# A two-part transformer block in one kernel: first units of both gated feed-forwards on unnormed chunks, grid attention with split values, cross attention with four score banks

## What is computed

```python
def modulate(h, shift, scale):
    return h * (1.0 + scale[:, None, :]) + shift[:, None, :]

def swiglu(h, w1, w3, w2):
    return (jax.nn.silu(h @ w1) * (h @ w3)) @ w2

for layer in range(2):
    mod = silu(c) @ ada_w[layer] + ada_b[layer]            # six vectors of 1024
    sh1, sc1, g1, sh2, sc2, g2 = jnp.split(mod, 6, axis=-1)
    h = modulate(rms_norm(x), sh1, sc1)
    y = pool_attention_mixer(h, ...) if layer == 0 else mlstm_mixer(h, ...)
    x = x + g1[:, None, :] * y
    h = modulate(rms_norm(x), sh2, sc2)
    x = x + g2[:, None, :] * swiglu(h, ffn_w1[layer], ffn_w3[layer], ffn_w2[layer])

# grid attention, in pool_attention_mixer: 8 query heads of 64, 2 key/value heads
s = einsum('bkgqd,bksd->bkgqs', q_blk, kt) * scale         # 128 queries x 512 keys
p = jax.nn.softmax(s, axis=-1)
o = einsum('bkgqs,bksd->bkgqd', p, vt)
# beside it: pooled means of 4 windows times w_pool; [pool, attention] @ w_out

# cross attention: 4 heads of 256
p = jax.nn.softmax(einsum('bshd,bmhd->bhsm', q, k) / sqrt(256), axis=-1)
o = einsum('bhsm,bmhd->bshd', p, v)
```

## Time and profile before

| | |
|---|---|
| median of 3 runs | 2150.06 us |
| lowest, highest | 2149.21, 2152.73 us |
| the profiled execution | 2150.77 us, of which the span is 2149.1 us |
| mean granted clock of TensorE | 0.983 of full speed |
| busy share of TensorE (matmuls), its weight loads | 97%, 79% |
| busy share of VectorE, ScalarE, GpSimd | 53%, 34%, 41% |
| DMA | 233 MB, mean 109 GB/s |

### The profile page before, as it was taken

How to read it: one execution, slowest core, us unless ns; L and a number is a source line. 1 busy time by engine, 2 the same in 40 slices (tenths; PEclk the granted TensorE clock), 3 DMA queues, 4 the chain that set the end, 5 groups by cost and what they waited for, 6 DMA issues and landing times.

```text
span 2149.1 us, 26665 instructions
## 1 busy us (share of the span) xinstructions
PE 2076.9 (97%) x10222; PEld 1695.0 (79%) x10222; DVE 1134.0 (53%) x1894; ACT 728.9 (34%) x985; POOL 878.2 (41%) x472
## 2 busy tenths in 40 slices
PE   6999899999999999998999999999999999999998
PEld 5877688888888888775578888887897777888887
DVE  4344565636878895468557665704665743111112
ACT  5343533324423223345533222123253333222121
POOL 2322432744444444333234444444445333444442
PEclk8999999999999999999999999999999999999999
DMA  4322202424455543330045555422332022223322
GB/s 139 109 74 85 69 1 79 142 93 136 139 176 196 175 160 96 98 104 29 12 155 167 196 171 182 136 89 69 118 120 89 30 79 79 98 88 102 100 81 79
DMA packets 225160, 233.26 MB, mean 109 GB/s; under 512 B 4227, under 2 KB 220116, under 8 KB 224924
## 3 DMA queue, kind: packets, MB, share of 16 engines
q1 hardware_dynamic: 224672, 231.70, 33.3%
q10 hardware_dynamic: 380, 0.11, 0.0%
HBM read 229.55 MB, written 2.24 MB: 108 GB/s over the span
## 4 chain that ended last, share of the span: by engine, by line
PE 86%; DVE 7%; ACT 2%; issue 2%; DMA 1%; POOL 1%; ACTq 0%; DVEq 0%
PE ps L2118 21%; PE ps L2120 21%; PE ps L2119 21%; PE ps L2167 6%; PE ps L2172 3%; PE ps L2805 2%; PE ps L2819 1%; PE ps L2274 1%; PE ps L2533 1%; POOL wL L593 1%; DVE hnL L1338 1%; DMA raw<-in_w_xkv_dram 1%; PE ps L2464 1%; ACT wH L725 1%; DVE T L1351 1%
## 5 line engine op out<-in xcount | busy, mean ns | idle before, releaser
L593 POOL TENSOR_TENSOR wL<-raw,wH 128x1024 fp32r<-128x1024 f32 (+2 forms) x322 | 773.8, 2425 | 1106.1 <-ACT wH L725 1088.7
L725 ACT ACTIVATE wH<-raw 128x2048 fp32r<-128x2048 f32 (+2 forms) x161 | 302.5, 1879 | 473.0 <-PE ps L2120 352.2
L2118 PE MATMUL ps<-hnH,wH 128*128 128x512 f32 x1152 | 455.9, 396 | 4.3 <-POOL wL L593 4.3
L2120 PE MATMUL ps<-hnH,wL 128*128 128x512 f32 x1152 | 449.9, 391 | 0.0
L2119 PE MATMUL ps<-hnL,wH 128*128 128x512 f32 x1152 | 448.9, 390 | 0.0
L2118 PE MATMUL ps<-uH,wH 128*128 128x512 f32 x712 | 281.8, 396 | 4.2 <-DVE uL L1336 1.8
L2120 PE MATMUL ps<-uH,wL 128*128 128x512 f32 x712 | 278.9, 392 | 0.0
L2119 PE MATMUL ps<-uL,wH 128*128 128x512 f32 x712 | 278.5, 391 | 0.0
L1710 DVE SCALAR_TENSOR_TENSOR adacc<-adaw,small,adacc 128x256 f32<-128x256 f32 x336 | 267.5, 796 | 12.3 <-DVE adacc L1710 0.3
L2118 PEld LDWEIGHTS ps<-hnH,wH 128*128 128x128 f32 x1152 | 217.1, 188 | 49.1 <-issue 5.7
L2120 PEld LDWEIGHTS ps<-hnH,wL 128*128 128x128 f32 x1152 | 216.5, 188 | 45.9
(11 more groups left out here) (413 smaller groups left out, 3021.7 us busy)
## 6 DMA issues: line engine op xcount, KB each, us to landing
raw<-in_ffn_w_dram SPq DMA_DIRECT2D x60, 1024.0 KB, 5.3
adaw<-in_ada_w_dram SPq DMA_DIRECT2D x48, 1024.0 KB, 7.3
raw<-in_w_dram SPq DMA_DIRECT2D x32, 1024.0 KB, 5.2
raw<-in_w_in_dram SPq DMA_DIRECT2D x14, 1024.0 KB, 5.5
raw<-in_od_w_in_dram SPq DMA_DIRECT2D x12, 1024.0 KB, 5.4
raw<-in_w_xkv_dram SPq DMA_DIRECT2D x8, 1024.0 KB, 5.4
raw<-in_ffn_w_dram SPq DMA_DIRECT2D x8, 768.0 KB, 4.3
raw<-in_ev_w_in_dram SPq DMA_DIRECT2D x5, 1024.0 KB, 5.4
```

The source lines that it names most:

```text
L593: nc.gpsimd.tensor_tensor(wL[n % 2][:, k0:k1, 0:c], raw[n % 2][:, k0:k1, 0:c], wH[n % 2][:, k0:k1, 0:c].bitcast(F32), ALU.subtract).then_i ...
L725: nc.scalar.activation(wH[n % 2][:, 0:kc, 0:c], raw[n % 2][:, 0:kc, 0:c], ACT.Copy).then_inc(w_hi, 1)
L2118: nc.tensor.matmul(out_ap, wh, xh, start=first, stop=False)
L2120: return nc.tensor.matmul(out_ap, wl, xh, start=False, stop=last)
```

## The change

Three parts, joined.

**Both gated feed-forwards.** The first unit (w1, columns 0 to 255) is multiplied with x (1 + scale), not normed, in `hnH` and `hnL`, made during the last units of `ev_out` or `od_out` (`raw`). The norm's sums and its broadcast run inside the unit. The shift's part of the product, shift @ w1, is kept apart: VectorE multiplies and adds the raw w1 unit over its eight chunks with the shift (`shift_products`, into `wacc`), TensorE sums over partitions into `ps[7]` (`shift_sums`, between the last two blocks of the stage before), and ScalarE adds it as the bias of Silu (`fconst`). The blocks are multiplied by the inverse root in `ssum`. SyncE waits for the products before it loads unit 2 into the same buffer. Normed chunks go to `uH`, `uL`, hidden ones to `hnH`, `hnL`. The loops over i are written out on SyncE, ScalarE, VectorE and TensorE. One piece of the conditioning moves from `ff2_0` into `ev_out`, and its sums are ordered anew.

**Grid attention.** Probabilities stay without their inverse sums; they are split into `gpH` (ScalarE) and `gpL` (VectorE, out of PSUM); the values are split too (`gvp`, padded with zeros to 128 columns), so that a value product is three fast matmuls over 128 columns, two heads adding into one bank. Inverse sums of two heads at a time are copied out by GpSimd (`gsx`), transposed by TensorE, copied by ScalarE (`gsc`), and VectorE multiplies the pair's output with them (`gout`).

**Cross attention.** Four score banks; scores wait for the exponential of step g - 4, and the first output product waits for the last one.

Tiles are placed anew for it (left out below). The diff, cut:

```diff
+SUMS_STEP = (11, 21, 29, 35)
+SUMS_BANK = (3, 0, 0, 3)
...
+CROSS_SCORES = (4, 5, 1, 2)
...
+                if layer == 0:
+                    load_ada(1, 0, 0)
+                for u in range(24):
+                    if u == 2:
+                        sp.wait_ge(wc_done, layer + 1)
+                    load(n0 + u)
+                    if layer == 0 and u < 11:
+                        load_ada(1, 0, u + 1)
+                    if layer == 0 and u >= 12:
+                        load_ada(1, 1, u - 12)
...
+            for half in range(2):
+                nc.gpsimd.memset(gvp[:, half, :, 0:64].bitcast(F32), 0.0)
+                nc.gpsimd.memset(gvp[:, half, :, 128:192].bitcast(F32), 0.0)
+                nc.gpsimd.memset(gvp[:, half, :, 256:320].bitcast(F32), 0.0).then_inc(g_pad, 1)
...
+                pool.wait_ge(g_inv, o + 1)
+                if o:
+                    pool.wait_ge(g_bc, o)
+                nc.gpsimd.tensor_copy(gsx.rearrange("p (i h c) -> p i h c", i=TB, h=2),
+                                      hrs[:, 8 * o:8 * o + 8].rearrange("p (h i x) -> p i h x", h=2, x=1).to_broadcast(
+                                          [P, TB, 2, 64])).then_inc(g_sx, 1)
+
+            inverse_sums(0)
             g = 0
             for grp, w in enumerate(WINDOWS):
+                if grp == 3:
+                    inverse_sums(1)
...
+                    if 0 <= t < ns:
+                        h, i = t // TB, t % TB
+                        act.wait_ge(tp_done, step0 + t + 1)
+                        if i == 0 and h >= 2:
+                            act.wait_ge(pv_done, ATT["grid"]["pv0"] + h - 1)
+                        nc.scalar.activation(gpH[h % 2][:, :, i * P:(i + 1) * P],
+                                             ps[6 + (step0 + t) % 2][:].rearrange("p (j t) -> p j t", j=TB),
+                                             ACT.Copy).then_inc(pt_done, 1)
+                    if s < ns:
+                        act.wait_ge(mx_done, g + 1)
+                        act.wait_ge(tp_done, g - PR_RING + 1)
+                        m = g % PR_RING
+                        nc.scalar.activation(pr[m][:], ps[4 + g % 2][:], ACT.Exp, bias=nmax[:, m:m + 1],
+                                             accum_out=hstat[:, s:s + 1]).then_inc(ex_done, 1)
+                    if s - 1 in SUMS_STEP:
+                        o = SUMS_STEP.index(s - 1)
+                        act.wait_ge(g_bc, o + 1)
+                        if o:
+                            act.wait_ge(g_out, o)
+                        nc.scalar.activation(gsc[:], ps[SUMS_BANK[o]][:], ACT.Copy).then_inc(g_sc, 1)
...
+                    if s >= 16 and s % 8 == 0:
+                        o = s // 8 - 2
+                        act.wait_ge(g_out, o + 1)
+                        nc.scalar.activation(uH[:, 4 + o, :], gout[:], ACT.Copy).then_inc(op_hi, 1)
...
+                high(n0 + 2)
+                for c in range(2):
+                    act.wait_ge(r_scaled, 2 * layer + c + 1)
+                    nc.scalar.activation(R[c][:], R[c][:], ACT.Silu, bias=fconst[:, c:c + 1]).then_inc(silu_done, 1)
+                for c in range(2):
+                    act.wait_ge(blk_taken, TAKEN[b0 + 2 + c + 1])
+                    nc.scalar.activation(hnH[:, c, :], T[(q0 + c) % 2][:], ACT.Copy).then_inc(op_hi, 1)
...
+                for i in range(2):
+                    for p in range(1 - i, 4):
...
+            def raw_norm(layer, n, first):
+                name, at = f"ff2_{layer}", layer * 48 + 24
+                highs_and_squares(n, name, BLOCK0[n], first, raw=(Q0[name + "_raw"], hnH, lambda j: modp[:, at + 8 + j:at + 9 + j]))
+                roots(name)
+                norm_highs(Q0[name + "_norm"], lambda j: mod[:, at + j:at + j + 1], to=uH)
...
+                        chain(nc.vector.tensor_reduce(nmraw[:, m:m + 1], ps[CROSS_SCORES[s % 4]][:, 0:M_MEM], AX, ALU.max))
...
+                    if 0 <= t < ns:
+                        h, i = t // TB, t % TB
+                        dve.wait_ge(pt_done, step0 + t + 1)
+                        if i == 0 and h >= 2:
+                            dve.wait_ge(pv_done, ATT["grid"]["pv0"] + h - 1)
+                        if t == TB:
+                            dve.wait_ge(g_ql, 4)
+                        ts = slice(i * P, (i + 1) * P)
+                        nc.vector.tensor_tensor(gpL[h % 2][:, :, ts], ps[6 + (step0 + t) % 2][:].rearrange("p (j t) -> p j t", j=TB),
+                                                gpH[h % 2][:, :, ts].bitcast(F32), ALU.subtract).then_inc(g_pl, 1)
...
+                    if s >= 9 and s % 8 == 1 and s < ns + 8:
+                        o = s // 8 - 1
+                        dve.wait_ge(ex_done, step0 + 8 * o + 8)
+                        if o < 4:
+                            nc.vector.reciprocal(hrs[:, 8 * o:8 * o + 8], hstat[:, 8 * o:8 * o + 8]).then_inc(g_inv, 1)
...
+                    if s >= 15 and s % 8 == 7:
+                        o = s // 8 - 1
+                        dve.wait_ge(pv_done, ATT["grid"]["pv0"] + 2 * o + 2)
+                        dve.wait_ge(g_sc, o + 1)
+                        if o:
+                            dve.wait_ge(op_lo, Q0["ev_mix"] + MIX_OUT[o - 1] + 1)
+                        nc.vector.tensor_tensor(gout[:], ps[1 + o % 2][:], gsc[:], ALU.mult).then_inc(g_out, 1)
...
+            nc.vector.tensor_copy(value_part(0), values_in).then_inc(v_hi, 1)
+            dve.wait_ge(v_hi, 1)
+            nc.vector.tensor_tensor(value_part(1), values_in, value_part(0).bitcast(F32), ALU.subtract).then_inc(v_row, 1)
...
+            grid_attention({0: lambda: take_pool(3), 4: lambda: queries_low(2), 7: lambda: queries_low(3),
...
+                dve.wait_ge(raw_in[n % 2], 16 * (n // 2 + 1))
+                for k in range(KC):
+                    if k == 0:
+                        chain(nc.vector.tensor_scalar(wacc[:], raw[n % 2][:, 0, :], shift(0), None, ALU.mult))
+                    else:
+                        ins = nc.vector.scalar_tensor_tensor(out=wacc[:], in0=raw[n % 2][:, k, :], scalar=shift(k), in1=wacc[:],
+                                                             op0=ALU.mult, op1=ALU.add)
+                        if k < KC - 1:
+                            chain(ins)
+                        else:
+                            ins.then_inc(wc_done, 1)
...
+            residual_and_sums(b, "ff2_0", mcol(mod, 0, 2), raw=(Q0["ff2_0_raw"], hnH, hnL, mcol(modp, 0, 4)),
+                              beside={2: lambda: conditioning(1, 0, 0), 5: lambda: shift_products(0)})
...
+                dve.wait_ge(wc_mm, layer + 1)
+                nc.vector.tensor_copy(fconst, ps[7][:, 0:2])
+                dve.wait_ge(bc_copied, 2 + layer)
+                for c in range(2):
+                    dve.wait_ge(blk_done, b0 + c + 1)
+                    nc.vector.tensor_tensor(R[c][:], ps[(b0 + c) % 4][:], ssum[:], ALU.mult).then_inc(r_scaled, 1)
+                for i in range(2):
                     for p in range(4):
+                        if i == 0 and p == 0:
+                            pair(0, 0)
+                            cond(0, 1)
+                            continue
                         cond(i, 2 * p)
                         cond(i, 2 * p + 1)
                         pair(p, i)
...
+                dve.wait_ge(bc_done, NORMS[name] + 1)
+                nc.vector.tensor_copy(ssum[:], ps[4][:]).then_inc(bc_copied, 1)
+                for _ in normed_steps(name, mcol(modp, layer, 4), Q0[name + "_norm"], mcol(mod, layer, 3), to=(uH, uL)):
...
-                    dst, ts = ps[4 + g % 2][:, 0:M_MEM], slice(i * P, (i + 1) * P)
-                    pe.wait_ge(ex_done, g - 1)
+                    dst, ts = ps[CROSS_SCORES[s % 4]][:, 0:M_MEM], slice(i * P, (i + 1) * P)
+                    pe.wait_ge(ex_done, g - 3)
+                    if s == 2:
+                        pe.wait_ge(blk_taken, TAKEN[BLOCK0[AT["xo"][0]]] - 2)
...
                         unit_ready(n)
+                        pe.wait_ge(ex_done, step0 + ns)
...
+                    pe.wait_ge(ex_done, g + 1)
+                    if t >= 2:
+                        pe.wait_ge(pt_done, g - 1)
+                        pe.wait_ge(g_pl, t - 1)
...
+                    for i in range(TB):
+                        ins = nc.tensor.transpose(ps[SUMS_BANK[o]][:, i * P:(i + 1) * P], gsx[:, i * P:(i + 1) * P], ident)
+                    ins.then_inc(g_bc, 1)
...
+                            pe.wait_ge(g_out, h // 2 - 1)
+                    c0 = h // 4 * P + (64 if h % 2 == 0 else 0)
+                    dst = ps[1 + h // 2 % 2]
+                    first, last = h % 2 == 0 and j == 0, h % 2 == 1 and j == TB - 1
+                    nc.tensor.matmul(dst[:], gvp[:, 0, j, c0:c0 + P], gpH[h % 2][:, j, :], start=first, stop=False)
+                    nc.tensor.matmul(dst[:], gvp[:, 0, j, c0:c0 + P], gpL[h % 2][:, j, :], start=False, stop=False)
```

(57 more changed lines are left out.)

135 lines of the change are left out of this document (102 added, 33 removed).

## The result

The changed kernel takes 2129.5 us, median of four runs (2125.9 to 2131.9), against 2151.1 (2149.2 to 2152.7) for the kernel before: a ratio of 0.9891, 95% interval 0.9873 to 0.9910.

A forecast was written before the change was run, and what follows sets the result against it. TensorE, busy 97% of the span, was taken as the bound. Gated feed-forwards -5.7 and -5.5, grid attention -2.3 and cross attention -1.0 summed to -14.5 us, giving a forecast median of 2135.5 us, range 2129 to 2144.

The forecast's parts named there:

- 32 x (1.00 - 0.68): Grid attention: replacing each float32 value product (1.00 us) by three fast matmuls (0.68) saves 10.2 us over 32 steps.
- the 0.11 of the scores: Grid attention: two score matmuls take 0.57 us instead of 0.45; the excess, a change of kind, only moves to the values.
- the 3 us for the clusters: Grid attention, steps 17 to 21 and 25 to 29: VectorE's work nearly equals TensorE's; 0 to 4 us each, 3 together.
- The start: Start of grid attention: queries moved ahead of a row maximum and a low part waiting for ScalarE cost 2 us (0 to 3).
- the end: End of grid attention: TensorE waits for high and low of the last transposes, not one copy, +0.8 us (0.3 to 1.5).
- Lies in idle time: Values in `ev_in`: their added low part (0.7 us) was claimed to fall in idle time, costing nothing.
- the cover: `ev_out`: shift products ready by 1101, asked for by TensorE at about 1102.4, leaving 1.4 us; lateness cost taken as 0.
- the term 25.74: Gated feed-forwards: the stretch of `ff1` in us, taken whole with its 1.1 us stall as base for both new stretches.
- (b): Rival: grid attention gains all of its matmul time, -7.8 us, giving 2130; chance 0.13.
- (a): Rival: VectorE bounds the grid attention clusters, so grid attention gains nothing or loses, +0 to +4, 2138 to 2142; chance 0.20.
- (c): Rival: the first unit does not cover the norm, half the gain of both feed-forwards stays, about 2141; chance 0.12.
- (d): Rival: slower than before; grid attention's 32 subtractions take 2.9 us instead of 0.7 beside GpSimd, 2164; chance 0.05.

## Why the prediction was wrong

*The grid step.* The step that failed is the term 32 x (1.00 - 0.68) for grid attention. It priced the product's own rows, moved the 0.11 of the scores to the values, and let the rest of the old step stand. The moving was right (0.46 and 0.79 forecast, 0.46 and 0.78 measured). The transposes, left at 0.53, take 0.35, and that is the 0.19 by which the step was off: it fell by 0.51 us and not by 0.32. What the runs show in its place: the old step carried a price of 0.34 us that hangs on a float32 product with 64 output rows and that its neighbours pay in part, so that it leaves with the product. The transposes take 0.53 us before such a product, 0.43 before a float32 one of 128 rows and 0.35 before a fast one. The rows had a sign of it: in the old step the last transpose takes 0.20 us to the next matmul and the three ahead of it 0.11 each.

*Where the 6 us of grid attention lie.* In the middle: from the start of the ninth step to the last score 52.4 us became 43.2, -9.2, where the forecast's terms make -2.8 there (23 value products of 0.32, three of the four broadcasts, the 3 us for the clusters). Of the difference, 23 x 0.19 = 4.4 us are the step. The start was right: the first eight steps went from 15.0 to 16.8 us, +1.8, with +2 forecast less one value product. So was the end, from the last score: 10.20 to 9.39, -0.8, where the forecast's terms make -1.2; TensorE's gaps there come to 1.2 us, 0.8 was taken.

*The clusters.* I allowed 3 us for VectorE at steps 17 to 21 and 25 to 29. A step with a pool product takes 2.45 us, 0.86 over its neighbour, as before (2.96 over 2.10): no loss. One step outside them, with the end of a head and `gout`, lost 0.8. The 3 were too many by about 2.

*The values' low part.* "Lies in idle time" was wrong. TensorE waits for it before a product of the head norms (L2915, idle 0.49):

```profile
960.44 1.95 PE L2915 MATMUL ps<-gs,cst 128*128 128x512 f32 x4 [0.49 <-DVE gvp L1978]
```

with the rest 0.7 us, in each kernel that has it.

*The first units.* The mechanism and the cover were right: no half clock, `wacc` ready at 1091.0 and asked for at 1091.63, so 0.6 us of cover where I had 1.4. Seven of the eight products went at the pace of the earlier trace rows; the last, beside GpSimd's `wL`, took 2.50 us. Mis-sized was the term 25.74, `ff1`'s stretch taken whole: some 1.7 us of it belong to its late residual and the clash behind that, by the two runs with a delayed residual, and both feed-forwards gained 1.7 us more than forecast. The hole before the third unit is 0.4, not 1 to 2.

*Cross attention* came as forecast (-1.1 for -1.0), and its remaining wait, 1.0 us, is for GpSimd's multiplication, as said.

*The rivals.* (b), all of the matmul time, gave 2130, and near that the medians fell (2129.5 to 2131.8). That was luck: its -7.8 for the grid rested on 0.32 a step with no losses, when 0.51 with losses came, and both feed-forwards gained more than it had. (a) and (c) did not occur. (d) fell: GpSimd is at work for 24.7 us of this stage, 15 of the 32 subtractions, with one input in PSUM, lie beside one of its operations, and none of the 32 took more than 0.69 us (line, names, count | busy, mean ns | idle before):

```profile
L1533 DVE TENSOR_TENSOR gpL<-ps,gpH 128x512 fp32r<-128x512 f32 x32 | 21.9, 685 | 4.0 <-ACT gpH L893 3.5
```

The low parts of the feed-forward, with two inputs in SBUF, were held until GpSimd's operation had ended. This is the rule of the Trainium skill ("SBUF — State Buffer", Who interferes with whom), and the runs here agree with both halves of it: 0.685 us against up to 2.58.

*The range.* Its low end took the bounds one by one, and for the grid the bound was the matmul time by my own pricing of the step, which let nothing but the product's own rows get shorter. That the neighbours might should have widened it downwards. For the feed-forwards the low end allowed 13 us together, and 14.6 came.

## What to carry to other kernels

When one operation of a tight loop is replaced, price the whole step anew from undisturbed rows of each kind (a fast matmul takes 0.227 us), and treat what is left of the old step as a price that may vanish with the operation replaced. A similar stage is a model only after its own late arrivals and clashes are taken out of it. And a long stall of TensorE is to be charged with the half clock that can follow it: here 2.5 us on top of a wait of 5.3.

## What the runs showed of the hardware

- A float32 matmul of 512 columns into 64 output rows costs more than into 128: with one of them (two records in the profile) in a step of grid attention the step is 2.11 us against 1.76 for 128 rows (2.10 against 1.76 in the old loop). For three fast products it makes no difference (1.59 and 1.59).
- After a wait of 5.3 us TensorE ran 5 us at granted clock 0.50 and lost 2.5 us beyond the wait.
- VectorE beside GpSimd: 15 subtractions with one input in PSUM took at most 0.69 us each; low parts with both inputs in SBUF, 0.69 to 0.75 us alone, took 1.28 to 2.58 us and ended 0.55 us behind GpSimd's operation.
- The same stretch of code ran at a granted clock of 0.76 in one execution and 1.00 in another, 14.3 against 11.2 us.
